# Two of the token tiles of a PEER layer computed densely over all experts, in an unrolled expert stage

## The reference, cut to what matters

```python
def retrieve(xb):                       # xb: 128 tokens x 1024
    qry = (xb @ w_q).reshape(PEER_BLOCK, PEER_HEADS, 2, PEER_HALF)      # 8 heads, 2 halves of 128
    scores = jnp.einsum('thpd,hpkd->thpk', qry, sub_keys)               # 128 keys in each half
    s_top, i_top = lax.top_k(scores, PEER_TOPK)                         # 16 of each half
    cand_s = s_top[:, :, 0, :, None] + s_top[:, :, 1, None, :]          # 256 pairs
    cand_i = i_top[:, :, 0, :, None] * N_KEYS + i_top[:, :, 1, None, :] # expert = 128 * i + j
    s_fin, pos = lax.top_k(cand_s, PEER_TOPK)
    idx = jnp.take_along_axis(cand_i, pos, axis=-1)                     # 16 experts per token and head
    gate = jax.nn.softmax(s_fin)
    act = jax.nn.gelu(jnp.einsum('thed,td->the', jnp.take(expert_u, idx, axis=0), xb))
    return jnp.einsum('the,thed->td', gate * act, jnp.take(expert_v, idx, axis=0))
```

## Time and profile before

| | |
|---|---|
| median of 3 runs | 6972.05 us (6964.3 to 6974.19) |
| span of the profiled execution | 6983.1 us (the page gives no other time for it) |
| TensorE busy | 5019.2 us (72%) |
| VectorE busy | 3459.6 us (50%) |
| GpSimd busy | 3478.8 us (50%) |
| ScalarE busy | 1330.8 us (19%) |
| moved by DMA | 1542.61 MB, 221 GB/s over the span |

### The profile page before, as it was taken

How to read it: one execution, slowest core, us unless ns; L and a number is a source line. 1 busy time by engine, 2 the same in 40 slices (tenths; PEclk the granted TensorE clock), 3 DMA queues, 4 the chain that set the end, 5 groups by cost and what they waited for, 6 DMA issues and landing times. The chain is left out here.

```text
span 6983.1 us, 61149 instructions
## 1 busy us (share of the span) xinstructions
PE 5019.2 (72%) x15179; PEld 2494.7 (36%) x15179; DVE 3459.6 (50%) x8674; ACT 1330.8 (19%) x2853; POOL 3478.8 (50%) x2949
## 2 busy tenths in 40 slices
PE   7788899985666666666666646888785666666665
PEld 2547566571222222222222225555552222222222
DVE  6545313226555555555555537241135555555553
ACT  4214212011111111111111111231111111111110
POOL 0511111215667676776777653012315767676765
PEclk9899999997999999999999978889988999999998
DMA  7200121116988999998989941013226999998986
GB/s 284 72 27 1 48 66 39 58 54 242 339 324 325 334 339 330 332 334 323 331 326 336 334 157 55 1 37 90 72 67 244 333 331 335 331 340 325 340 330 250
DMA packets 568298, 1542.61 MB, mean 221 GB/s; under 512 B 53929, under 2 KB 185465, under 8 KB 568185
## 3 DMA queue, kind: packets, MB, share of 16 engines
q0 software_dynamic: 374080, 1361.51, 53.4%
q1 hardware_dynamic: 194112, 179.79, 8.4%
HBM read 1538.92 MB, written 2.20 MB: 221 GB/s over the span
## 5 line engine op out<-in xcount | busy, mean ns | idle before, releaser
L1844 PE MATMUL ps<-vr,dg 128*128 128x512 f32 x5248 | 2758.5, 653 | 1289.3 <-DMA vr<-in_expert_v_dram,icv 1188.7
L1752 DVE SCALAR_TENSOR_TENSOR ur<-ur,hx 128x1024 f32<-128x1024 f32 x1280 | 1569.1, 1226 | 1584.9 <-DMA ur<-in_expert_u_dram,icu 1534.2
L1844 PEld LDWEIGHTS ps<-vr,dg 128*128 128x128 f32 x5248 | 952.8, 201 | 3043.9 <-issue 2145.6
L1586 POOL DMA_INDIRECT vr<-in_expert_v_dram,icv x1312 | 1486.9, 1133 | 881.0 <-DVE icv L1760 405.6
L1595 POOL DMA_INDIRECT ur<-in_expert_u_dram,icu x1280 | 1362.0, 1064 | 423.8 <-issue 371.3
L1812 ACT ACTIVATE dg<-ident,wt 128x128 f32<-128x128 f32 x1312 | 463.2, 394 | 1931.4 <-PE ps L1844 1520.0
L1944 PE MATMUL ps<-hi,w_hi 128*128 128x512 f32 (+1 forms) x832 | 296.5, 356 | 67.0 <-POOL w_lo L405 57.2
L937 POOL MEMSET pr<- 128x768 f32 x4 | 2.9, 737 | 598.8 <-POOLq L84 598.8
L1945 PE MATMUL ps<-lo,w_hi 128*128 128x512 f32 (+1 forms) x832 | 294.7, 354 | 0.0
L1946 PE MATMUL ps<-hi,w_lo 128*128 128x512 f32 (+1 forms) x832 | 294.0, 353 | 0.0
L1159 PE MATMUL ps<-wt,hT 128*128 128x512 f32 x640 | 281.0, 598 | 0.6 <-DMA wt<-in_w_in_dram 0.6
(11 more groups left out here) (290 smaller groups left out, 5992.2 us busy)
## 6 DMA issues: line engine op xcount, KB each, us to landing
wt<-in_w_mod_dram SPq DMA_DIRECT2D x24, 2048.0 KB
wt<-in_w_in_dram SPq DMA_DIRECT2D x32, 1024.0 KB
vr<-in_expert_v_dram,icv POOLq DMA_INDIRECT x1312
ur<-in_expert_u_dram,icu POOLq DMA_INDIRECT x1280
wt<-in_w_in_dram SPq DMA_DIRECT2D x32, 512.0 KB
wg<-in_w_in_dram SPq DMA_DIRECT2D x32, 512.0 KB
wt<-in_peer_wq_dram SPq DMA_DIRECT2D x32, 512.0 KB
wp<-in_p_a_dram SPq DMA_DIRECT2D x16, 512.0 KB
```

The source lines that it names most:

```text
L1586: gp.indirect_dma_start(vr[:, j % RV, :], None, tab_v, bass.IndirectOffsetOnAxis(ap=icv[:, par, j:j + 1], axis=0)).then_inc(v_in[j % RV], 16)
L1752: ve.scalar_tensor_tensor(out=ur[:, j % RU, :].unsqueeze(1), in0=ur[:, j % RU, :].unsqueeze(1), scalar=1.0, in1=hx[:, bass.ds(n // H + t0, ...
L1844: mm = pe.matmul(ps[:, 2 * par + q, :], dg[:, j % RD, :], vr[:, j % RV, q * BANK:(q + 1) * BANK], start=(j == 0), stop=(j == TOPK - 1))
```

## The change

**Tiles.** The last two tiles of each layer (`dt`) are no longer gathered. The others (`gt`) are: 4 tiles, 32 heads, 512 units in the first layer; 2 tiles, 16 heads, 256 units in the second. `NU` is the number of units, `TU` = 128 the units of a tile.

**The dense tiles.** Their experts are selected too (calls of kind "d"). The results (first key, second key, gate, for 8 heads x 16) lie in `sel`, are turned by TensorE, and for each token a 128 x 128 matrix of gates is built: VectorE makes one-hot matrices (`one_hots`), TensorE multiplies them, ScalarE copies to `st`, SP stores to DRAM (`g_dram`, 16.8 MB a layer). There are 64 builds of 4 tokens. Then for each of 128 blocks of 128 experts, for all 256 tokens at once: load the block of a turned copy of `expert_u` (512 KB) and the block of `expert_v` (512 KB); S, 8 matmuls of 256 columns; gelu on ScalarE; `weighted`, times the gates read back, on VectorE; O, 4 matmuls of 512 columns which add up in PSUM over all blocks.

```diff
+    u = inputs["expert_u"]
+    ut = _np.ascontiguousarray(u.reshape(u.shape[0], P, P, KD, P).transpose(0, 1, 4, 3, 2))
+                def one_hots(b):
+                    ve.wait_ge(turn_out, b // (NB // 2) + 1)
+                    if b >= 2:
+                        ve.wait_ge(built, b - 1)
+                    t0 = b * GPB
+                    ve.tensor_tensor(out=oh[:, b % 2], in0=iota[:].unsqueeze(1).broadcast_to((P, GPB, P)),
+                                     in1=selT[:, 1, t0:t0 + GPB].unsqueeze(2).broadcast_to((P, GPB, P)), op=ALU.is_equal).then_inc(hot_ready, 1)
+                    for i in range(GPB):
+                        ve.tensor_scalar(og[:, b % 2, i, :], iota[:], selT[:, 0, t0 + i:t0 + i + 1], selT[:, 2, t0 + i:t0 + i + 1],
+                                         ALU.is_equal, ALU.mult).then_inc(hot_ready, 1)
+                def weighted(i):
+                    ve.wait_ge(act_done, i + 1)
+                    if i >= 3:
+                        ve.wait_ge(o_done, i - 2)
+                    if i % KB == 0:
+                        ve.wait_ge(gb_in[i // KB % 2], 16 * (i // KB // 2 + 1))
+                    ve.tensor_tensor(out=ww[:, i % 3, :].rearrange("p (s t) -> p s t", t=32), in0=sg[:, i % 3, :].rearrange("p (s t) -> p s t", t=32),
+                                     in1=gb[:, i // KB % 2, :, i % KB, :], op=ALU.mult).then_inc(ww_ready, 1)
```

TensorE's program, whole:

```diff
+                for g in range(END):
+                    x = g - LAG
+                    if x >= 0:
+                        if x % TU == 0 and x:
+                            pe.wait_ge(y_out, 2 * (x // TU))
+                        pe.wait_ge(dg_ready, x + 1)
+                        pe.wait_ge(v_in[x % RV], 16 * (x // RV + 1))
                         for q in range(2):
+                            mm = pe.matmul(ps[:, q, :], dg[:, x % RD, :], vr[:, x % RV, q * BANK:(q + 1) * BANK],
+                                           start=(x % TU == 0), stop=(x % TU == TU - 1))
                         mm.then_inc(v_used, 1)
...
+                    for b in build_at.get(g, ()):
+                        pe.wait_ge(hot_ready, (b + 1) * (1 + GPB))
+                        if b >= 4:
+                            pe.wait_ge(build_out, b - 3)
+                        for i in range(GPB):
+                            mm = pe.matmul(ps[:, 4 + b % 4, i * P:(i + 1) * P], oh[:, b % 2, i, :], og[:, b % 2, i, :], start=True, stop=True)
+                        mm.then_inc(built, 1)
+                    for i in s_at.get(g, ()):
+                        pe.wait_ge(ud_in[i % RDU], 16 * (i // RDU + 1))
+                        if i >= 2:
+                            pe.wait_ge(act_done, i - 1)
+                        else:
+                            pe.wait_ge(turn_out, 2)
+                        for k in range(KD):
+                            mm = pe.matmul(ps[:, 2 + i % 2, 0:TOK2], ud[:, i % RDU, k, :], xT[:, k, :], start=(k == 0), stop=(k == KD - 1))
+                        mm.then_inc(s_done, 1)
+                    for i in o_at.get(g, ()):
+                        pe.wait_ge(ww_ready, i + 1)
+                        pe.wait_ge(vd_in[i % RDV], 16 * (i // RDV + 1))
...
+                        for d in range(2):
+                            for q in range(2):
+                                mm = pe.matmul(ps[:, 4 + 2 * d + q, :], ww[:, i % 3, d * P:(d + 1) * P], vd[:, i % RDV, q * BANK:(q + 1) * BANK],
+                                               start=(i == 0), stop=(i == NE - 1))
+                        mm.then_inc(o_done, 1)
```

**When.** Every engine walks the same list of units. The first selections and the builds come early, the dense blocks after them, spread evenly up to the end:

```diff
+        LAG = TOPK + 2
+        END = NU + LAG
+        RU = RV = 6
+        PER_STEP, BUILDS = (2, 2) if len(gt) > 2 else (4, 2)
...
+        turn_unit = [soft_unit[d_call[H * (d + 1) - 1]] + 1 for d in range(2)]
+        build_at = {}
+        at = 0
+        for b in range(NB):
+            at = max(at, BUILDS * (turn_unit[b // (NB // 2)] + 1))
+            build_at.setdefault(at // BUILDS, []).append(b)
+            at += 1
+        builds_end = (at - 1) // BUILDS
+        DENSE0 = builds_end + 2
+        DENSE1 = NU + 8
+        unit_of = [DENSE0 + i * (DENSE1 - DENSE0) // NE for i in range(NE)]
+        for i, g in enumerate(unit_of):
+            s_at.setdefault(g, []).append(i)
+            w_at.setdefault(g + 1, []).append(i)
+            o_at.setdefault(g + 2, []).append(i)
```

```diff
+                for g in range(END):
+                    if g < NU:
+                        if g % TOPK == 0:
+                            gp.wait_ge(idx_ready, g // TOPK + 1)
+                        if g >= RU:
+                            gp.wait_ge(dot_done, g - RU + 1)
                         gp.sem_inc(gathers, 1)
+                        gp.indirect_dma_start(ur[:, g % RU, :], None, tab_u, bass.IndirectOffsetOnAxis(ap=idx[:, g:g + 1], axis=0)).then_inc(u_in[g % RU], 16)
+                    x = g - LAG
+                    if x >= 0:
+                        if x >= RV:
+                            gp.wait_ge(v_used, x - RV + 1)
+                        gp.sem_inc(gathers, 1)
+                        gp.indirect_dma_start(vr[:, x % RV, :], None, tab_v, bass.IndirectOffsetOnAxis(ap=idx[:, x:x + 1], axis=0)).then_inc(v_in[x % RV], 16)
```

**The scores** are made in `queries`, four keys' halves of a tile in one bank, copied by VectorE and stored to DRAM (`sc_dram`) by SP:

```diff
+                def scores(hp):
+                    pe.wait_ge(q_out, 4 * (hp + 1))
+                    for i, t in enumerate(tiles):
+                        m = hp * nt + i
+                        if m >= 4:
+                            pe.wait_ge(score_out, m - 3)
+                        for j in range(4):
+                            n = 4 * hp + j
+                            mm = pe.matmul(ps[:, 4 + m % 4, j * P:(j + 1) * P], qT[:, n % 8, t * P:(t + 1) * P], kT[:, n, :], start=True, stop=True)
+                        mm.then_inc(scored, 1)
...
+                    if n % 4 == 0 and n:
+                        scores(n // 4 - 1)
+                scores(PAIRS - 1)
```

More of the change, by code:

```diff
@@ L1405, in queries @@
         NG = 2 * H
+        tiles = list(range(t0, NT))
+        nt = len(tiles)
+        PAIRS = H // 2
         pieces = [(0, CTX), (CTX, T)] if t0 == 0 else [(CTX, T)]
-        npc = len(pieces)
         with ctx:
@@ L1422, in _, with load @@
                 sp.dma_start(keys[:], a["peer_keys"][l].rearrange("h t k d -> k (h t) d")).then_inc(k_in, 16)
[L1424 to L1432, removed]
+                def load(n):
+                    sp.dma_start(wt[:, n % UN], wcols(a["peer_wq"][l], n * P, P)).then_inc(w_in[n % UN], 16)
@@ new lines, in store @@
+                def store(hp):
+                    for i, t in enumerate(tiles):
+                        m = hp * nt + i
+                        sp.wait_ge(score_out, m + 1)
+                        sp.dma_start(self.sc_dram[t, :, hp * BANK:(hp + 1) * BANK], so[:, m % 4, :]).then_inc(stored[m % 4], 16)
+                for n in range(UN):
+                    load(n)
+                for n in range(NG):
+                    if n + UN < NG:
+                        sp.wait_ge(w_split, n + 1)
+                        load(n + UN)
+                    if n % 4 == 1 and n >= 5:
+                        store(n // 4 - 1)
@@ L1439, in _ @@
             @block.vector
             def _(ve):
[L1441 to L1448, removed]
+                for n in range(NG):
+                    ve.wait_ge(w_in[n % UN], 16 * (n // UN + 1))
+                    if n >= 2:
+                        ve.wait_ge(w_used, n - 1)
+                    ve.tensor_copy(w_hi[:, n % 2], wt[:, n % UN]).then_inc(w_hi_ready, 1)
+                    ve.wait_ge(w_hi_ready, n + 1)
+                    ve.tensor_tensor(out=w_lo[:, n % 2], in0=wt[:, n % UN], in1=w_hi[:, n % 2].bitcast(F32), op=ALU.subtract).then_inc(w_split, 1)
+                    if n % 4 == 1 and n >= 5:
+                        score_evict(ve, n // 4 - 1)
@@ L1851, in body @@
[L1851 to L1857 removed]
+                    for d in range(2):
+                        if g == turn_unit[d]:
+                            pe.wait_ge(sel_ready, H * (d + 1))
+                            pe.wait_ge(gated, d_call[H * (d + 1) - 1] + 1)
+                            for j in range(3):
+                                mm = pe.transpose(ps[:, 2 + d, j * P:(j + 1) * P], sel[:, d, j, :], self.ident[:])
+                            mm.then_inc(turned, 1)
```

584 lines of the change are left out of this document (327 added, 257 removed).

## The result

The changed kernel takes 6781.69 us, the median of 4 runs (6765.61 to 6798.34), against 6973.12 (6964.3 to 6984.02) of the kernel before on the same chip: a ratio of 0.9722, 95% interval 0.9701 to 0.9743. The profiled span is 6784.5 us for 6983.1, 198.6 less.

A forecast was written before the change was run, and what follows sets the result against it. Drained queues and transfers bound each head; afterwards VectorE, then TensorE would. Terms -310 + 39 + 54 - 10 = -227 on a span of 6983.1 gave 6756, less 11.05 us to the median: 6745 us, range 6560 to 6990.

The forecast's parts named there:

- the likeliest mechanism: Whole kernel: the forecast case, 6640 to 6860 us, chance 0.55, with VectorE bounding early phases and TensorE the dense phase.
- the step from span to median: Whole kernel: the profiled span lies 11.05 us above the median of runs, so 6756 becomes 6745 us.
- The head: Expert stage before the change: 51.3 us a head, 43.6 of transfers at 385 GB/s and some 7.7 of drained queue.
- A and B: Expert phases before dense blocks (extra selections, builds): VectorE bounds them, 474 and 86 us in layer 0, 351 and 86 in layer 1.
- C: Dense-block phase of each expert stage: TensorE bounds it, 1515 us in layer 0 and 1187 in layer 1.
- The rival of a GpSimd held up at each issue: Gathers in the expert stages: each issue waits for one VectorE operation, +400 us, 7145 us in all; chance 0.04.
- A loss of 5% for hand-overs: Dense phase: TensorE loses 5% to hand-overs between three engines, 76 us in layer 0 and 59 in layer 1.
- The gates' chain: Start of the dense phase: last store of `st`, gates and first `vd` follow one another, 8 us a layer.
- Between stages: Outside the expert stages: `queries` and its end add 54 us over both layers, `modulate_rows` takes off 10.
- The sum: Whole span: -310 for layer 0, +39 for layer 1, +54 for `queries`, -10 for `modulate_rows`, -227 us in all.
- The granted clock of TensorE: Rival in the dense phase: TensorE's mean clock falls, at 0.85 costing 341 us more than forecast, 7085 us; chance 0.10.
- The starved middle: Rival in the expert stages: hand-overs cost 10% in the dense phase, 5% before it; 6930 us, chance 0.16.

The follow-up runs named there:

- experiment 5: Changed kernel, all tiles gathered, GpSimd waiting at each head for issued u rows: ratio 0.9732 with 6 and 6 buffers; with 8 and 4, 0.9771 (0.9226 without the wait).
- 8/4: Changed kernel with all tiles gathered, no added wait, 8 buffers for u rows and 4 for v rows: ratio 0.9226 to the kernel before.
- 6/4: Changed kernel with all tiles gathered, 6 buffers for u rows and 4 for v rows: ratio 0.9194 to the kernel before.
- experiment 1: Changed kernel with ScalarE making each diagonal one unit earlier, ahead of the block's gelu: ratio 0.9407 to the kernel before, span 6584.3 us.
- experiment 8: Changed kernel with diagonals one unit ahead and 6 and 4 buffers, dense tiles in both layers: ratio 0.9474 to the kernel before.

## Why the prediction was right, and where not

Forecast 6745, measured 6782, inside the range, on the side that it favoured; the likeliest mechanism was the one that decided. Of the 37 us, 28 are in the sum (a span of 6756 predicted, 6784.5 measured) and 8 in the step from span to median, for which 11.05 us were taken off, where the changed kernel's span lies 2.8 above its median. By its steps:

- *The head.* 43.6 us of transfers and 7.7 of drained queue. The dips at heads' ends are gone where all tiles are gathered without the wait (a DMA share of 1.01 over 1700 us with 8 and 4 buffers), and experiment 5 puts the drain at 4.7 us a head. The rest of the 7.7, some 3 us, went with the hardware loop, the copies and the addition into `y`; no run tells these apart. Transfers at 385 GB/s are right where the queue is kept full as in experiments 8/4 and 6/4 (390 and 394), but with the changed kernel's 6 and 6 buffers all tiles gathered hold 364.
- *A and B, VectorE-bound.* From the start of the stage to the first S, 22 + 474 + 86 = 582 us were predicted in layer 0 and 573 measured, 459 and 440 in layer 1. VectorE was to be over 90% busy in A, and was (90 and 94%). The DMA share was to be below 0.85: it was in layer 1 (0.71 and 0.75), not in layer 0 (0.89 and 0.90). There 324 GB/s at a share of 0.89 make 364 at a full one, and C's 322 at 0.90 make 358, not 385: charging the hardware queue's packets by their bytes alone was too cheap. It cost no time, since the transfers bound neither phase. The rival of a GpSimd held up at each issue did not come. Its row for the first window of A in layer 0 (ns min/median/max):

```profile
L1683 POOL DMA_INDIRECT ur<-in_expert_u_dram,idx x67: 942/949/2015, 1643.4 to 1841.2; - x67
```

Half of the issues took 949 ns or less, beside a VectorE that is 92% busy; the longest took 2 us. The Trainium skill ("SBUF — State Buffer", Who interferes with whom) states that VectorE and GpSimd share a port pair under an exclusive lock. The rival had a wait at every issue; the trace shows a longer issue only now and then, and does not say what that one waited for.
- *C, TensorE-bound.* An S pass of 0.21 us: the timeline has 15 weight loads in 3.21 us, 0.214 each. C of layer 1, with loss and tail: 1187 + 59 + 8 + 3 = 1257 predicted, 1258 measured. C of layer 0: 1515 + 76 + 8 + 3 = 1602 predicted, 1666 measured. **This is the term that was mis-sized.** A loss of 5% for hand-overs was taken for a number without a place. In the runs it is one place: 107 waits in layer 0, 91.4 us in all; the one shown above is 0.76 us in the records, and 0.95 in the rhythm of the matmuls (S begins at 3788.39, 16 passes of 0.214 end at 3791.82, the next begins at 3792.77). In layer 1 there are 45 of them: blocks stand closer there (128 in 173 units), the O of an earlier block often follows S in the same unit, and TensorE has that to do meanwhile. 107 x 0.95 = 102 us, of the 120 that C of layer 0 got back in experiment 1; 45 x 0.95 = 43 of 52. Experiment 1 leaves 1545 us in C of layer 0 for 1515 + 8 + 3, a loss of 19 us, 1.3%, once the order is mended. Read from the diff, the order of two instructions on ScalarE was there to be seen: a gelu that waits for S, ahead of a diagonal that waits for nothing.
- *The gates' chain*, 8 us: VectorE waited longer for the gates, 19.9 us in layer 0, but only 8.0 of it reached TensorE, before the first O; in layer 1 4.2.
- *Between stages.* The work ahead of layer 0's expert stage grew by 22 us (26 predicted), that between the stages by 13 (18 predicted). `queries` is bound by TensorE, as said, at 97% busy for the 93% of the earlier trace rows:

```profile
1435.00:1598.00 163.00, 158.40 (x974) 142.48 (x975) 45.99 (x55) 16.40 (x36) 0.00 (x0) 0.98 0.30 89
```

- *The sum.* Layer 0's stage 2238 us (2184 predicted, 2494 before), layer 1's 1698 (1716; 1677 before). -256 + 21 + 22 + 13 + 1 = -199.
- *Rivals.* The granted clock of TensorE was low in A (0.77 and then 0.94 in layer 0, 0.63 and 0.90 in layer 1), where in the first window of each layer TensorE is busy 54% and 33% of the time and VectorE is the bound, and stayed at 0.99 and 1.00 in C, near its upper level of 2.4 GHz: no loss. The starved middle had its mechanism right in part (a hand-over that costs 10% in C of layer 0: 1666 for 1515), and none of its 5% in A and B.

What the forecast had right in size it had wrong in credit. It booked 227 us to the dense tiles. The experiments divide it otherwise: all that the change does beside the dense tiles (the queue that is never drained above all) is worth 0.0774 of the time with the buffers as they were (0.9226), of which the change gives back some 200 us by the ScalarE order (experiment 1), and the rest by dense tiles that gain nothing in layer 0 and cost 216 us in layer 1 (experiment 8). The 6 and 6 buffers cost where the gathers are the bound; with the dense tiles and the order mended, 6 and 4 gain nothing over them.

The Trainium skill ("DMA: Bandwidth & Descriptors", Specifications) gives about 358 GB/s as a core's limit from HBM, a stack's rate divided by its two cores. Here one core runs and moves 394 GB/s over 1700 us, so the measurement decides.

## What to carry over

When a change both removes a stall and adds an algorithm, price and run the stall's removal by itself: here it was worth more than the whole. On an engine that runs in order, look in the diff for each instruction that waits for a long producer ahead of one that waits for nothing, and price it as so many times so long instead of a per cent of the phase. Buffers are not free cover: two fewer for the `v` rows gained 3% where the gathers were the bound, and nothing where TensorE was, so their split is worth a run.

## What was not expected of the hardware

- The gathers of 4 KB rows hold 390 to 394 GB/s at a DMA share of 1.01 over 1700 us, when 10 or 12 buffers are split 6/4 or 8/4, and 364 GB/s at 0.97 when they are split 6/6.
- With 6/6, VectorE stands still for up to 4.1 us for no releaser that the trace can name, some 100 us in 1700; with 6/4 and 8/4 there is no such wait in the same window.
- Where TensorE is the bound, blocks of 512 KB loaded by the hardware queue beside the gathers cost no time: leaving 65 MB a layer of them out took C of layer 0 from 322 to 281 GB/s and changed the time by less than 1 us there (3422.7 us for 3422.9, to the start of layer 1's stage). Whether they slow gathers that are the bound themselves was not tried.
